# A two-layer hybrid step on Trainium2: the second unit's first experts found in two halves of eight, the samples' gate moved between the halves of the first unit, and query products cut in two

## The chip, the cores and the metric

One core of a Trainium2 chip runs the whole program. The metric is the device time of one execution in microseconds (us); lower is better.

## The reference

Two layers run over 256 prompt tokens and 8 sample tokens, 1024 features each. A layer is a state-space branch and an attention branch mixed by two gates, and then a retrieval of single experts ("PEER"). Cut to what matters here:

```python
x = x + (ga * ya + gb * yb) @ w_out
h = rmsnorm(x, norm_ffn)
for head in range(8):
    q = h @ wq[head]                       # 256 columns, two halves of 128
    s1, s2 = q[:, :128] @ keys[head, 0].T, q[:, 128:] @ keys[head, 1].T
    sc1, i1 = top_k(s1, 16); sc2, i2 = top_k(s2, 16)
    cand = sc1[:, None] + sc2[None, :]      # 16 x 16 sums
    sc, sel = top_k(cand, 16)
    idx = i1[sel // 16] * 128 + i2[sel % 16]
    act = gelu(sum(u[idx] * h)) * softmax(sc)
    out += act @ v[idx]
x = x + out
```

The rows u[idx] and v[idx] stand side by side in one table, 2048 float32 numbers (8 KB) for one expert.

## The kernel before

All five engines run straight programs written out by hand, one layer after the other; semaphores are the only order between them. No planner is at work. In a layer come first the projections, the state-space scan and the attention. Then comes the expert stage, which this change is about.

**Slots.** The expert stage is cut into units: one (token tile, head) pair of 128 tokens each, eight heads for tile 0, eight for tile 1, and one short unit for the samples. A unit has 16 slots, the last one 8, so that a layer has 264 slots. For slot n, POOL issues one gather (line 2506) that brings one expert row for each of 128 tokens, 1 MB in all, into place n % 8 of a ring of 8 (`ring`). DVE multiplies the u half with the tokens and sums (`inputs`, line 1843), ACT takes the gelu of the 128 sums (line 2228), DVE builds a small diagonal matrix from it (`diagonal`, line 1852), and PE adds diagonal times v half to sums that stay in PSUM banks for a whole tile (`outputs`, line 1195). The gather of slot n waits until `outputs(n - 8)` has run. DVE's loop takes the work of slot n in this order: `inputs(n)`, `diagonal(n - 1)`, at a unit's start `weights(u)`, then some steps of the generator `best_experts(u + 1)`, which finds the 16 experts of the next unit, then what `late_tiles(n)` holds.

**What else runs beside the slots.** The query products of the heads and their scores against the keys stand in a table of steps, `projection_steps` (line 77). Behind `outputs(n)` PE runs `STEPS[n]`: `queries` (8 matmuls with 264 columns, line 530), `scores` (line 1082) or `rows` (transposes of the normed rows of tile 1 and of the samples, line 539). ACT copies their result from PSUM in its own slot loop, behind `gelu(n)`, from `STEPS[n - 2]`, or `STEPS[n - 4]` for n under 8. So ACT, and with it gelu(n + 1) and `diagonal(n + 1)`, waits where PE is not through with the product. Where both have 4 PSUM banks each, `wide` are those that ACT empties and `aux` those that DVE empties.

**The start of the stage.** The first unit cannot be prepared beside slots. DVE finds its experts alone in `first_experts` (lines 1731 to 1759): eight from the best 8 x 8 candidates, whose number lets slot 0 start, then eight more from 16 x 16. Then it adds `out(0, 1)` to tile 1, forms the samples' gate (`sample_gated`, lines 1585 and 1587), adds `out(1, 1)` and copies the samples' partial sums (line 1242). PE needs the gate for `out_samples` (line 1042), behind which come `out(2, 1)`, the two sums over the samples' parts (line 1141) and `out(3, 1)`. POOL's gathers of slots 4 and 5 wait for `out_samples(0)`, those of slots 6 and 7 for `out(2, 1)` and `out(3, 1)`, whose weights lie where these slots' rows go. `outputs(0)` waits until DVE has read all of these banks, in its slot 4. In slots 6 and 7 DVE forms the norm of tile 1 and of the samples (`px_mean`, and `px_rows`, line 1672); the steps `rows` on PE wait for it. The second unit's experts come from the general `best_experts(1)`, whose 16 numbers appear together, in slot 11.

## Time and profile before

| what | value |
|---|---|
| median of 3 runs | 2105.01 us (2101.08 to 2106.8) |
| the profiled execution | 2099.31 us |
| its span, first to last instruction | 2097.5 us |
| PE, DVE, ACT, POOL busy | 79%, 69%, 23%, 32% |
| gathers (line 2506) | 528 of 1 MB |
| mean DMA rate over the span | 356 GB/s |
| mean granted TensorE clock | 0.823 |

The span is cut into stages by what DMA carries. A layer's expert stage starts with its first gather, at 361.2 us in layer 0 and at 1402.7 us in layer 1, and ends some 14 us behind its last gather, issued at 1031.3 us and at 2072.7 us. Busy shares over the whole span mix these stages with the others, so the stage has to be looked at by itself, window by window.

### The profile page before, as it was taken

What the parts mean: (1) busy time and instruction counts of PE and PEld (TensorE: products, weight loads), DVE (VectorE), ACT (ScalarE), POOL (GpSimd) and SP (SyncE); (2) the same over time, 40 slices, a digit from 0 to 9 for tenths busy, and PEclk for the clock granted to TensorE, in tenths of its full rate; (3) what the DMA queues carried; (4) which work ended last, traced back from release to release, by engine and by line L of the source; (5) the groups of instructions that cost most, each with busy time, mean ns of one, the idle gap of its engine ahead of it and who ended that gap; (6) DMA issues with size and microseconds to landing.
All of it is one profiled execution on the core that took longest, in us unless ns stands there. A gap on an engine that the chain in (4) does not pass through costs nothing. (4 is left out here: it accounts for less than half of the span.)

```text
span 2097.5 us, 29681 instructions
## 1 busy us (share of the span) xinstructions
PE 1662.4 (79%) x10874; PEld 839.5 (40%) x10874; DVE 1446.4 (69%) x3630; ACT 489.6 (23%) x1422; POOL 676.2 (32%) x614
## 2 busy tenths in 40 slices
PE   7999999878787666666699999998787776666665
PEld 6888677433333111111178876764332321111110
DVE  3557544778778878778736565347887888787787
ACT  2346211211211221111222543112112112111112
POOL 0011000354544454444300110014444454444442
PEclk9999999887887676666799999998887876666667
DMA  5568897999999999999954688978999999999997
GB/s 181 189 205 302 302 393 279 351 397 421 415 421 421 405 421 421 420 417 412 383 175 155 215 323 293 389 288 351 405 417 416 417 420 409 421 421 418 417 415 319
DMA packets 136004, 746.76 MB, mean 356 GB/s; under 512 B 16692, under 2 KB 17309, under 8 KB 57763
## 3 DMA queue, kind: packets, MB, share of 16 engines
q0 software_dynamic: 84416, 587.50, 68.8%
q1 hardware_dynamic: 51442, 157.37, 20.9%
q8 instruction: 86, 1.41, 0.3%
q14 instruction: 60, 0.48, 0.1%
HBM read 733.48 MB, written 11.52 MB: 355 GB/s over the span
## 5 line engine op out<-in xcount | busy, mean ns | idle before, releaser
L1195 PE MATMUL ps<-arena 64*64 64x512 f32 x4096 | 750.6, 832 | 371.0 <-DVE arena L1852 369.4
L2506 POOL DMA_INDIRECT arena<-in_peer_uv,arena x528 | 628.3, 1190 | 777.4 <-PE ps L1195 619.5
L1843 DVE CUSTOM_DVE_ANT_0 arena<-arena,h 128x1024 f32<-128x1024 f32 x512 | 627.1, 1225 | 216.0 <-DMA arena<-in_peer_uv,arena 208.9
L1195 PEld LDWEIGHTS ps<-arena 64*64 64x64 f32 x4096 | 140.8, 166 | 919.0 <-DVE arena L1852 864.8
L530 PE MATMUL ps<-ht_tok,wring 128*128 128x264 f32 (+1 forms) x1472 | 346.8, 395 | 4.2 <-DMA wring<-in_w_in 2.8
L2228 ACT ACTIVATE arena<-arena 128x1 f32<-128x1 f32 x528 | 105.2, 203 | 969.9 <-DVE arena L1843 968.3
L530 PEld LDWEIGHTS ps<-ht_tok,wring 128*128 128x128 f32 x1472 | 281.2, 194 | 68.8 <-issue 15.8
L1852 DVE TENSOR_SCALAR arena<-consts,arena 128x64 f32<-128x64 f32 (+1 forms) x528 | 164.6, 312 | 38.8 <-ACT arena L2228 35.3
L530 PE MATMUL ps<-arena,wring 128*128 128x264 f32 x256 | 63.9, 393 | 3.2 <-DVE arena L1522 3.2
L530 PE MATMUL ps<-ht_tok,arena 128*128 128x264 f32 (+2 forms) x280 | 60.4, 373 | 1.4 <-DVE ht_tok L1715 1.4
L530 PE MATMUL ps<-arena,gate 128*128 128x256 f32 x256 | 59.1, 383 | 0.0
L530 PEld LDWEIGHTS ps<-ht_tok,arena 128*128 128x128 f32 x280 | 47.6, 208 | 25.5 <-issue 17.8
L2483 POOL DMA_DIRECT2D nrow<-in_norm_ffn x2 | 1.1, 534 | 175.2 <-PE ps L897 175.2
L2228 ACT ACT_TABLE_LOAD x40 | 51.3, 1283 | 0.9
L530 PEld LDWEIGHTS ps<-arena,gate 128*128 128x128 f32 x256 | 47.2, 189 | 9.8 <-issue 3.4
L530 PEld LDWEIGHTS ps<-arena,wring 128*128 128x128 f32 x256 | 46.2, 190 | 11.1 <-DVE arena L1522 3.5
L2469 POOL DMA_DIRECT2D out<-h x16 | 8.5, 534 | 119.9 <-DVE h L1435 119.9
L530 PE MATMUL ps<-wring,ht_tok 128*128 128x272 f32 (+2 forms) x192 | 42.8, 379 | 1.7 <-DVE ht_tok L2553 1.7
L2221 ACT ACT_TABLE_LOAD x34 | 43.6, 1283 | 0.8
L1843 DVE DVE_READ_ACCUMULATOR2_ANT arena<- 128x1 f32 x528 | 43.4, 82 | 0.0
L2192 ACT COPY gate<-ps 128x264 f32<-128x264 f32 (+2 forms) x40 | 13.4, 335 | 126.1 <-PE ps L530 126.1
L530 PEld LDWEIGHTS ps<-wring,ht_tok 128*128 128x128 f32 x192 | 34.7, 201 | 10.9 <-issue 3.4
(388 smaller groups left out, 1738.2 us busy)
## 6 DMA issues: line engine op xcount, KB each, us to landing
arena<-in_pages SPq DMA_DIRECT2D x256, 272.0 KB, 6.2
wring<-in_w_in SPq DMA_DIRECT2D x36, 1024.0 KB, 5.1
arena<-in_peer_uv,arena POOLq DMA_INDIRECT x528, 12.5
h<-in_state_ssm POOLq DMA_DIRECT2D x16, 512.0 KB, 6.4
out<-h POOLq DMA_DIRECT2D x16, 512.0 KB, 6.1
wring<-in_w_ssm_proj SPq DMA_DIRECT2D x8, 1024.0 KB, 11.4
arena<-in_w_out SPq DMA_DIRECT2D x8, 1024.0 KB, 8.7
arena<-in_peer_wq SPq DMA_DIRECT2D x6, 1024.0 KB, 10.6
```

The source lines that it names most:

```text
L530: last = pe.matmul(dst, w(c), rhs(c), start=start and c == 0, stop=stop and c == chunks - 1)
L1195: last = pe.matmul(ps[to:to + 64, SUM_BANK[t] + i, :], diag[rows, n % DIAGS, 0:64], ring[rows, HOME[n % RING], cols], start=n in TILE_FIRS ...
L1843: dve.tensor_tensor_reduce(ring[:, HOME[k], 0:D_MODEL], ring[:, HOME[k], 0:D_MODEL], tokens, 1.0, 0.0, ALU.mult, ALU.add, dots[:, column(n ...
L1852: dve.tensor_scalar(diag[:, n % DIAGS, 0:outs], table[:, 0:outs], gel[:, column(n)], wexp[:, column(n)], ALU.mult, ALU.mult).then_inc(sem( ...
L2192: wide.emptied(act.copy(gate[:, 2 * hh + m, lo:hi], ps[:, b, 0:hi - lo]))
L2221: act.activation(w, w, ACT.Exp, accum_out=wsum[:, u % 2:u % 2 + 1]).then_inc(sem("experts_exp"), 1)
L2228: act.activation(gel[:, at:at + 1], dots[:, at:at + 1], ACT.Gelu).then_inc(sem("gelu_ready"), 1)
L2469: pool.dma_start(h1[b], places[b % PLACES]).then_inc(sem(f"state_store{b % PLACES}"), 16)
L2483: pool.dma_start(nrow[:, :], of_layer("norm_ffn", layer).partition_broadcast(P)).then_inc(sem("ffn_row_load"), 16)
L2506: pool.indirect_dma_start(ring[:, HOME[k], :], None, table, bass.IndirectOffsetOnAxis(ap=idx[:, TOPK * u + j:TOPK * u + j + 1], axis=0)).t ...
```

## The change

It does five things.

1. `first_experts` becomes a generator, `early_experts(u)`, used for units 0 and 1. For unit 0, `out(0, 1)` and `sample_gated` run between its two halves. The copies of line 1242 move into DVE's slots 0 and 1.
2. On PE the two sums over the samples' parts (`samples_summed`) run behind `outputs(0)`, so that `out(3, 1)` follows `out(2, 1)` directly, and `outputs(0)` waits for `out(3, 1)` alone. DVE adds `out(2, 1)` and `out(3, 1)` in its slots 2 and 3, the samples' sums in slot 4. The banks of the tiles' sums change to fit.
3. Unit 1's experts are found as unit 0's: eight, whose numbers release slots 16 to 23, then eight more for slots 24 to 31. DVE takes 6 steps in slots 8 and 9 and 4 in each slot from 10 to 31, except none in 16 to 18; it was 4 in slots 7 to 11, then 3.
4. The first steps on PE stand later: head 1's queries behind slots 2 and 3 (were 0 and 1), its scores behind 4 (2), `rows` behind 11 to 13 (8 to 10), head 2's queries behind 14 and 15 (12 and 13) and its scores behind 17 (15). `px_mean` moves from DVE's slot 6 to 7, `px_rows` from 7 to 10. ACT reads `STEPS[n - 3]` for n under 8.
5. Each query product of heads 3 to 7 is cut in two: four of its eight matmuls behind the slot where the product stood, the other four behind the next. ACT copies the result one slot later. The scores stay behind the slot they had.

The core of the diff:

```diff
-SUM_BANK = (4, 6, 4)
+SUM_BANK = ((5, 6), (7, 4), (5, 6))
...
-    steps = {0: [("queries", 1, 0, 0, P)], 1: [("queries", 1, 1, 0, P)], 2: [("scores", 1, (0,))]}
+    steps = {2: [("queries", 1, 0, 0, P)], 3: [("queries", 1, 1, 0, P)], 4: [("scores", 1, (0,))]}
     for first in range(3):
-        steps[8 + first] = [("rows", first)]
+        steps[11 + first] = [("rows", first)]
...
-        at = (2, 6, 10) if hh > 2 else (12, 13, 15)
+        at = (2, 6, 10) if hh > 2 else (14, 15, 17)
+        for m in range(2):
+            if hh > 2:
+                steps[begun + at[m]] = [("queries_begun", hh, m)]
+            steps[begun + at[m] + (hh > 2)] = [("queries", hh, m, 0, TOKENS)]
...
+            def queries_begun(hh, m):
+
+                w = query_weights(hh, m)
+                b = wide.fill()
+                product(ps[:, b, 0:TOKENS], w, lambda c: ht[:, c, :], DC // 2, stop=False)
...
+                if n == 0:
+                    samples_summed()
...
-            first_experts()
-            out(0, 1)
-            sample_gated()
+            for said in early_experts(0):
+                if said == "first found":
+                    out(0, 1)
+                    sample_gated()
             out(1, 1)
-            ahead = best_experts(1)
-            for half in range(2):
-                copy4(hp[2][:, half * 512:(half + 1) * 512])
+            ahead = early_experts(1)
...
-                elif n == 6:
+                elif n == 7:
                     px_mean(1, slice(46, 48))
-                elif n == 7:
+                elif n == 10:
                     px_rows((1, 2))
...
-                for _ in range(0 if n < 7 or n in (TOPK, TOPK + 1) else 4 if n < 12 else 3):
+                for _ in range(0 if n < 8 or TOPK <= n < TOPK + 3 else 6 if n < 10 else 4 if n < 2 * TOPK else 3):
                     next(ahead, None)
...
-                for step in STEPS.get(n - 2 if n >= 8 else n - 4, ()):
+                for step in STEPS.get(n - 2 if n >= 8 else n - 3, ()):
...
-                if n in (0, TOPK // 2):
+                if u < 2 and n % (TOPK // 2) == 0:
                     pool.wait_ge(sem("idx_ready"), since("idx_ready") + 1 + n // (TOPK // 2))
                 elif j == 0:
-                    pool.wait_ge(sem("idx_ready"), since("idx_ready") + u + 2)
+                    pool.wait_ge(sem("idx_ready"), since("idx_ready") + u + 3)
```

The first place is on PE in layer 0, from the samples' parts to the first transposes of later rows. Four matmuls of line 1195 (1221 in the changed file) are one slot; 128x128 with one line of their own are the transposes, 8 or 2 in a row are queries and scores. Before:

```order
L1042 MATMUL ps<-arena,gate 32x256 x32
L530 MATMUL ps<-arena,gate 128x256 x8
L1141 MATMUL ps<-h,consts 8x512 x2
L530 MATMUL ps<-arena,gate 128x256 x8
L1195 MATMUL ps<-arena 64x512 x4
L530 MATMUL ps<-ht_tok 128x128 x8
L1195 MATMUL ps<-arena 64x512 x4
L530 MATMUL ps<-ht_tok 128x128 x8
L1195 MATMUL ps<-arena 64x512 x4
L1082 MATMUL ps<-arena,gate 128x128 x2
L1195 MATMUL ps<-arena 64x512 x24
L539 MATMUL ps<-consts,h 128x128
```

After the change:

```order
L1044 MATMUL ps<-arena,gate 32x256 x32
L532 MATMUL ps<-arena,gate 128x256 x16
L1221 MATMUL ps<-arena 64x512 x4
L1168 MATMUL ps<-h,consts 8x512 x2
L1221 MATMUL ps<-arena 64x512 x8
L532 MATMUL ps<-ht_tok 128x128 x8
L1221 MATMUL ps<-arena 64x512 x4
L532 MATMUL ps<-ht_tok 128x128 x8
L1221 MATMUL ps<-arena 64x512 x4
L1103 MATMUL ps<-arena,gate 128x128 x2
L1221 MATMUL ps<-arena 64x512 x28
L541 MATMUL ps<-consts,h 128x128
```

The second `out` product joins the first, the two 8x512 sums stand behind slot 0, head 1's products move by two slots, and seven slots instead of six stand between head 1's scores and the first transposes, which are then behind slot 11.

The second place is on DVE, around the norm of tile 1 and of the samples (line 1672, 1702 in the changed file), which the transposes need; line 1843 (1886) is a slot's input product and line 1852 (1895) its diagonal. Before:

```order
L1843 ISA arena<-arena,h 128x1024
L1843 ISA arena 128x1
L1852 TENSOR_SCALAR arena<-consts,arena 128x64
L1774 MAX arena<-arena 128x8 x2
L1778 MAX_INDEX arena<-arena 128x8 x2
L1783 MATCH_REPLACE arena<-arena 128x128 x2
L1774 MAX arena<-arena 128x8 x2
L1670 RECIPROCAL st<-st 128x2
L1672 SCALAR_TENSOR_TENSOR h<-x,st,nrow 128x1024 x2
L1843 ISA arena<-arena,h 128x1024
L1843 ISA arena 128x1
L1852 TENSOR_SCALAR arena<-consts,arena 128x64
```

After the change:

```order
L1776 MAX arena<-arena 128x8 x2
L1780 MAX_INDEX arena<-arena 128x8 x2
L1783 TENSOR_SCALAR arena<-arena,layer_off 128x8
L1784 CAST arena<-arena 128x8
L1786 TENSOR_TENSOR arena<-arena 128x256
L1788 MATCH_REPLACE arena<-arena 128x256
L1791 MAX arena<-arena 128x8
L1700 RECIPROCAL st<-st 128x2
L1702 SCALAR_TENSOR_TENSOR h<-x,st,nrow 128x1024 x2
L1886 ISA arena<-arena,h 128x1024
L1886 ISA arena 128x1
L1895 TENSOR_SCALAR arena<-consts,arena 128x64
```

Before, the norm stands behind four steps of the second unit's search, in slot 7; now it stands in slot 10, behind the whole first half of that search (slots 8 and 9) and four steps of its second half.

The third place is on PE, from head 2's scores (128x128 x4) to head 3's scores. Before:

```order
L1082 MATMUL ps<-arena,gate 128x128 x4
L1195 MATMUL ps<-arena 64x512 x12
L530 MATMUL ps<-ht_tok,arena 128x264 x8
L1195 MATMUL ps<-arena 64x512 x16
L530 MATMUL ps<-ht_tok,arena 128x264 x8
L1195 MATMUL ps<-arena 64x512 x16
L1082 MATMUL ps<-arena,gate 128x128 x4
```

After the change:

```order
L1103 MATMUL ps<-arena,gate 128x128 x4
L1221 MATMUL ps<-arena 64x512 x4
L532 MATMUL ps<-ht_tok,arena 128x264 x4
L1221 MATMUL ps<-arena 64x512 x4
L532 MATMUL ps<-ht_tok,arena 128x264 x4
L1221 MATMUL ps<-arena 64x512 x12
L532 MATMUL ps<-ht_tok,arena 128x264 x4
L1221 MATMUL ps<-arena 64x512 x4
L532 MATMUL ps<-ht_tok,arena 128x264 x4
L1221 MATMUL ps<-arena 64x512 x12
L1103 MATMUL ps<-arena,gate 128x128 x4
```

The number of matmuls is the same; a slot's four stand between the two halves of each product.

## Rows read from the trace of the kernel before

**Rows 1.** The page, part 2: mean busy share of the DMA engines in 40 slices, in tenths

```profile
DMA  5568897999999999999954688978999999999997
```

**Rows 2.** Windows: start:end, length, busy us (count) of PE, PEld, DVE, ACT, POOL, clock, DMA, GB/s

```profile
368.00:372.00 4.00, 4.00 (x48) 2.12 (x44) 0.76 (x2) 0.67 (x1) 0.82 (x1) 0.57 1.00 397
378.00:386.00 8.00, 7.40 (x46) 5.13 (x48) 7.01 (x17) 0.61 (x4) 2.70 (x3) 1.00 0.78 272
408.00:418.00 10.00, 10.00 (x41) 4.36 (x41) 7.18 (x18) 4.36 (x10) 6.71 (x5) 0.59 0.71 252
430.00:452.00 22.00, 16.64 (x92) 8.42 (x96) 19.14 (x52) 2.24 (x11) 9.40 (x7) 0.92 1.01 422
452.00:464.00 12.00, 7.95 (x64) 2.31 (x56) 9.50 (x28) 4.50 (x11) 9.87 (x9) 1.00 0.91 331
1449.00:1457.00 8.00, 8.00 (x33) 2.60 (x33) 6.32 (x16) 4.36 (x10) 4.91 (x4) 0.50 0.67 242
```

**Rows 3.** Timeline of POOL: gathers of slots 8, 16, 32, 34 [idle <-releaser]

```profile
384.79 0.94 POOL L2506 DMA_INDIRECT arena<-in_peer_uv,arena  x1 [1.29 <-PE ps L1195]
...
408.74 1.68 POOL L2506 DMA_INDIRECT arena<-in_peer_uv,arena  x1 [8.73 <-DVE arena L1816]
...
453.58 1.90 POOL L2506 DMA_INDIRECT arena<-in_peer_uv,arena  x1 [0.30 <-issue]
...
457.87 1.67 POOL L2506 DMA_INDIRECT arena<-in_peer_uv,arena  x1 [0.30 <-issue]
```

**Rows 4.** Line 2506, windows 453:454 and 457:458: issue to landing of slots 32 and 34

```profile
DMA to landing us min/median/max: 6.5/6.5/6.5
...
DMA to landing us min/median/max: 8.6/8.6/8.6
```

**Rows 5.** Timeline of PE, same columns, layer 0

```profile
367.79 5.35 PE L1042 MATMUL ps<-arena,gate 128*32 128x256 f32 x64 [2.45 <-DVE gate L1587]
...
401.38 1.99 PE L1195 MATMUL ps<-arena 64*64 64x512 f32 x8 [2.61 <-DVE arena L1852]
403.30 1.91 PE L539 MATMUL ps<-consts,h 128*128 128x128 f32 x6
...
415.65 4.08 PE L530 MATMUL ps<-ht_tok,wring 128*128 128x264 f32 x16
...
445.26 4.63 PE L530 MATMUL ps<-ht_tok,arena 128*128 128x264 f32 x16
...
473.56 5.83 PE L530 MATMUL ps<-ht_tok,arena 128*128 128x264 f32 x16
```

**Rows 6.** Timeline of DVE, same columns, layer 0

```profile
357.07 0.49 DVE L1740 MAX8 arena<-arena 128x8 f32<-128x128 f32 x2 [5.75 <-ACT arena L2205]
...
366.80 0.23 DVE L1759 TENSOR_SCALAR arena<-arena 128x16 f32<-128x16 f32 x1
...
391.18 0.49 DVE L1774 MAX8 arena<-arena 128x8 f32<-128x128 f32 x2 [0.74 <-ACT arena L2205]
...
393.73 2.48 DVE L1672 SCALAR_TENSOR_TENSOR h<-x,st,nrow 128x1024 f32<-128x1024 f32 x2
...
408.39 1.22 DVE L1843 CUSTOM_DVE_ANT_0 arena<-arena,h 128x1024 f32<-128x1024 f32 x1
...
409.76 1.22 DVE L1843 CUSTOM_DVE_ANT_0 arena<-arena,h 128x1024 f32<-128x1024 f32 x1
...
428.13 0.49 DVE L1774 MAX8 arena<-arena 128x8 f32<-128x128 f32 x2 [1.39 <-ACT arena L2205]
...
444.06 1.22 DVE L1843 CUSTOM_DVE_ANT_0 arena<-arena,h 128x1024 f32<-128x1024 f32 x1
...
450.44 0.32 DVE L1852 TENSOR_SCALAR arena<-consts,arena 128x64 f32<-128x64 f32 x1 [2.41 <-ACT arena L2228]
```

**Rows 7.** Timeline of ACT around the exponents of the second unit

```profile
409.51 1.28 ACT L2221 ACT_TABLE_LOAD   x1
410.81 0.22 ACT L2221 ACTIVATE arena<-arena 128x16 f32<-128x16 f32 x1
```

More of the change, by code:

```diff
@@ L1045, in out_samples, with query_part, query_weights @@
                 marks["sums", pair] = marks["sums"] = aux.n
-            def queries(hh, m, lo, hi):
+            def query_part(hh, m, c):
+                w = state["wq", hh]
+                rows = w[:, c] if hh != 6 else wq_high[:, c] if c < 3 else wq_late[:, c - 3]
+                return rows[:, m * P:(m + 1) * P]
+            def query_weights(hh, m):
                 if m == 0:
@@ L1137, in tensor_layer, with samples_summed @@
             out(2, 1)
-            pe.wait_ge(sem("aux_free"), since("aux_free") + 4 + marks["sums"])
-            for half in range(2):
-                b = aux.fill()
-                aux.filled(pe.matmul(ps[0:SAMPLES, b, :], cst("sel8"), hp[2][:, half * 512:(half + 1) * 512], start=True, stop=True))
             out(3, 1)
             marks["x", 1] = aux.n
+            def samples_summed():
+                pe.wait_ge(sem("aux_free"), since("aux_free") + 4 + marks["sums"])
+                for half in range(2):
+                    b = aux.fill()
+                    assert b not in SUM_BANK[0]
+                    aux.filled(pe.matmul(ps[0:SAMPLES, b, :], cst("sel8"), hp[2][:, half * 512:(half + 1) * 512], start=True, stop=True))
+                marks["x", 2] = aux.n
             def next_rows(t):
@@ L1750, in first_experts @@
                         then(dve.match_replace(sums, ctop[:, 0:8], sums, -3e38))
+                    yield
                     eight = slice(8 * k, 8 * k + 8)
                     then(dve.max(ctop[:, eight], sums))
+                    yield
                     then(dve.max_index(ctopi[:, eight], ctop[:, eight], sums))
-                    first_rows(k, n)
+                    yield
+                    yield from eight_rows(u, k, n)
+                    yield
                     if k == 0:
@@ L2237, in late_tiles @@
                 if n == 5:
-                    act.wait_ge(sem("aux_free"), since("aux_free") + 4 + marks["x", 1])
+                    act.wait_ge(sem("aux_free"), since("aux_free") + 4 + marks["x", 2])
                     squares(hp[1], x[:, 1, :], st[:, 46:47])
```

65 lines of the change are left out of this document (40 added, 25 removed).

## The prediction

> **What bounds the kernel now.** I read the page's slices first. Where the expert stage runs, the DMA engines are busy for nine tenths or more of nearly every slice, and the slices at the stage's start are lower [rows 1]. So the time of this stage is the bytes that its gathers bring, at the rate that DMA reaches, plus the holes in which DMA has too little queued. The windows size both. In an undisturbed stretch DMA moves 422 GB/s at a share of 1.01 (window 430:452) [rows 2], so a gather of 1 MB takes 2.48 us. Against that rate three stretches of layer 0 lack transfer: 378 to 386 moves 272 GB/s, a loss of 8 x (1 - 272/422) = 2.8 us; 408 to 418 moves 252, a loss of 4.0; 452 to 464 moves 331, a loss of 2.6 [rows 2]. That is 9.4 us in a layer. Layer 1 shows the same holes, such as 3.4 us in 1449 to 1457 [rows 2]. Everything that the change touches lies in this start of the stage. Past slot 34 nothing is to be had, and what the change can bring at most is 2 x 9.4 = 19 us.
>
> Then I read who makes each hole. For the first it is PE: slot 4's gather waits for the first of the samples' parts, which PE began at 367.79 after 2.45 us of waiting for the gate, and slot 8's leaves only at 384.79 [rows 3, 5]. For the second it is DVE: slot 16's gather waits 8.73 us for the index list [rows 3]. For the third it is PE, with a query product of 4.63 us in front of slot 23's output (445.26); ACT waits for it and DVE for ACT, 2.41 us at 450.44 [rows 5, 6]. The question is whether a hole closes or moves, so I follow each chain up to slot 34, which lands at 457.87 + 8.6 = 466.5 today [rows 3, 4].
>
> **Gate and first experts.** The gate no longer waits for the second half of the first unit's search. It is ready at some 362.3, and PE goes from `out(1, 1)` straight on at 365.4, 2.4 sooner. The samples' parts took 5.35 us in a stretch with a granted clock of 0.57 [rows 2, 5], that is partly at 1.2 GHz, after the wait that now goes. Their cost lies between 5.35 and, at 2.4 GHz throughout, 5.35 x 0.57 = 3.1. I take 3.7, since PE comes out of continuous work. The two sums behind slot 0 take 1.9 us more off the way. `outputs(0)` can then start at about 377, and gather 8 leaves near 378.5, 6 us sooner. The first hole closes, since DMA then always has a gather to work on, and at 2.48 us each slots 6, 7 and 8 land near 383, 385.5 and 388. At this point the change is 2.8 us ahead. `out(0, 1)` and the gate delay the second eight experts by 0.9 us. Their gathers leave 20 us later, so that costs nothing.
>
> **Slots 5 to 8.** Head 1's products are two slots later, so the earlier slots bring little here. The mean of tile 1's squares follows slot 7's input, which waits for its landing, and ACT then goes through two table loads of 1.28 us [rows 7] before it copies head 1's scores. I get 391.0 for DVE's first search step, against 391.18 [rows 6]. What could be gained by being sooner is spent here. The rows show no pause behind a table load: the load at 409.51 ends at 410.79 and the exponential starts at 410.81 [rows 7]. The Trainium skill (ScalarE: Activation LUTs, "What ACT_TABLE_LOAD costs") has some 1.38 us of drain on top of 1.28 us for each switch. By that, four switches in this stretch and at the second unit's exponentials would put 5.5 us more on each layer, about 2119 in all; this trace shows none of it, and I go by the rows.
>
> **The second unit's search.** Today DVE works without a pause from 391.18 to 409.76: five slots of 1.37 us (the distance of 408.39 and 409.76), the norm with its reciprocal, 2.65, the rest, 9.1, for the search [rows 6]. Searched in two halves as unit 0 (357.07 to 366.80) it costs 9.8 [rows 6], 0.7 more. With slot 8's input done while DVE waits, the new stretch is 391.0 + 4 x 1.37 + 2.65 + 9.8 = 408.9 up to slot 13, where today it is at 409.76. The first eight numbers come in slot 9, near 396.5, so gather 16 leaves when slot 8's output is through, about 397 in place of 408.74 [rows 3]. The second hole is gone, and DMA is nearly 7 us ahead.
>
> **What is late next.** The norm now comes in slot 10. Behind it stand two slots (2.7) and seven of the 24 steps (2.9) before 408.9, so it ends near 403.4. Today it ends at 396.2 [rows 6]. PE has almost nothing to do between. The transposes wait for slot 11's diagonal (about 408) and its output, and begin at some 410.0, against 403.30 [rows 5]. From there to the second unit's scores in DVE's hands it is 428.13 - 403.30 = 24.8 us today, with seven outputs in it [rows 5, 6]. Now there are six. I take off 1.5 (an output is 1.99 for two records at the low clock, 1.1 at the high one) and add 0.8, since gelu(12) waits for the second unit's exponentials, which come a slot later. That gives 434.1 for the third unit's search, 6.0 later than 428.13. DVE has then one slot more behind it: 15.9 us from there to slot 24's input today, 14.5 now. Slot 24's input starts at 448.6 against 444.06 [rows 6]. DVE, not DMA, sets slots 18 to 24, and the lead of 7 us is gone.
>
> **The cut products.** No matmul is added, and ACT waits less, as the result is read a slot later. In front of slot 23's output stand now some 2 us of product instead of 4.63. Slot 22's output ends near 449.6, half a product at 451.7, slot 23's output at 452.8, the other half at 454.7, slot 24's output at 455.8. Gather 32 leaves at 456.0, 2.4 later than 453.58 [rows 3], and lands 6.5 later [rows 4] at 462.5, against 460.1. Its followers are ready at once. If they follow without the hole of today, slot 34 lands at 467.5, 1.0 late; if the hole stays, 2.4 late. I take 1.5. The later cut products (slots 34 to 86) run while DMA has gathers queued at its full rate, and cost and bring nothing. If that queue were short, each would be worth up to the 2.41 of row 450.44. The moved banks, the one more wait of POOL and the later read of head 2's weights (head 7's load follows it by 50 slots) are hidden by the same queue.
>
> **Sum.** +1.5 us in each layer, +3 in all: 2099.3 + 3 = 2102.3 for an execution like the profiled one. That one is 5.7 under the median of 2105.0. On the median's scale I predict **2108**. A measurement of this kernel can tell about 0.3%, 6.3 us, from no change.
>
> **Rival 1: no measurable change (likeliest).** The chain above, with errors of 3 us a layer: 2102 to 2114. For it speaks that PE and DVE carry nearly the same work between slots 8 and 24 as before, and that DMA is starved whatever they finish late.
>
> **Rival 2: faster, 2093.** PE does its outputs and transposes between 405 and 421 at the high clock. Five outputs at 1.1 in place of 1.99 give 4.4 us, and 5.1 us of transposes at half the time 2.5, so the third unit's search starts near 427, ahead of today's. Gather 32 then leaves near 449 and lands near 455.5, and slot 34 near 460.5 instead of 466.5: -6 a layer, -12 in all, 2105 - 12 = 2093. Against it: the stretch has a clock of 0.59 today [rows 2] although PE is busy throughout.
>
> **Rival 3: slower, 2115.** PE rests longer ahead of the transposes than today (from 396 to 408 three outputs), so the low clock lasts into head 2's products. At the low clock a pair of those products costs 5.83 instead of 4.08 (the pairs at 473.56 and 415.65) [rows 5]. Two of them add 3.5 us to the search's start, every one of which reaches gather 32, as the queue is empty by then. 1.5 + 3.5 = 5 a layer, +10 in all: 2115. It decides from the point at which the third unit's search starts after 436. The Trainium skill (TensorE: Matmul & The Clock Gate, "Part 1: The HAM clock gate") says that the default state is throttled and that activity releases it; this rule speaks against making PE wait, and the windows agree, with 1.00 in 378:386 and 0.50 to 0.59 behind PE's rests.
>
> **How the numbers follow.** No change 0.44, faster 0.28, slower 0.28. Beyond the three mechanisms there are the bounds: the samples' parts at 5.35 cost 1.7 us that the wait for slot 7 hides; closing all holes would give 2086, which needs DVE and PE to gain 5 us that I don't find. The range for eight in ten is 2092 to 2119; the likeliest case alone has 2102 to 2114.
>
> **What would show it.** Right: slot 8's gather near 378.5 and no hole at 378 to 386; gather 16 near 397; the norm of line 1672 (now 1702) ending near 403.5; the first transposes near 410; the third unit's search near 434; gather 32 near 456; DMA shares under 0.95 spread between 413 and 460. Wrong: a third search that starts before 430, a clock near 1 from 408 on, or DMA at 420 GB/s from 386 to 470.

## The result and the profile after

| | before | changed |
|---|---|---|
| median of 15 runs each | 2103.06 us (2098.87 to 2107.66) | 2110.66 us (2105.24 to 2115.44) |
| ratio to before | | 1.0035, 95% interval 1.0025 to 1.0044 |
| the profiled execution | 2099.31 us | 2111.16 us |
| its span | 2097.5 us | 2109.1 us |

The changed kernel is slower by 7.6 us. This is just outside the 0.3% that I called no change, and the interval lies on both sides of that bound. The two profiled executions differ by 11.9 us, which is more than the medians do, since the one of before was a short one.

The slices of the changed kernel look as before at the start of the stage in layer 0, where one slice is lower [rows 1]:

```profile
DMA  5468897989999999999954689979999999999997
```

The windows tell more. The columns are those of [rows 2]:

```profile
378.00:386.00 8.00, 6.57 (x44) 2.86 (x44) 6.50 (x13) 2.18 (x6) 4.60 (x4) 1.00 1.01 425
396.00:408.00 12.00, 4.46 (x24) 0.61 (x16) 11.55 (x37) 1.69 (x3) 3.08 (x3) 0.59 1.02 421
408.00:418.00 10.00, 9.69 (x37) 3.29 (x37) 8.01 (x22) 3.19 (x9) 3.69 (x3) 0.50 0.88 344
418.00:430.00 12.00, 12.00 (x56) 7.42 (x56) 3.40 (x8) 0.97 (x4) 3.61 (x3) 0.83 0.77 268
430.00:445.00 15.00, 10.63 (x72) 5.13 (x72) 11.23 (x42) 2.04 (x8) 4.68 (x5) 1.00 1.00 402
445.00:452.00 7.00, 4.33 (x20) 1.81 (x13) 6.90 (x14) 0.61 (x3) 1.98 (x2) 0.56 0.80 294
452.00:464.00 12.00, 11.72 (x85) 5.17 (x83) 7.40 (x18) 4.84 (x12) 5.80 (x5) 0.97 0.74 253
```

The first hole is closed: 425 GB/s in place of 272. The second hole has moved rather than gone. DMA is at full rate to 408 and then lacks, against 422 GB/s, 10 x (1 - 344/422) = 1.8 us, 12 x (1 - 268/422) = 4.4 us, and later 0.7, 2.1 and 4.8 us. That is 13.8 us, against the 9.4 of the three holes before. So some 4 us of transfer time more are lost in this layer than before, and they are lost after slot 16.

Who makes these holes stands in the timelines, with columns as in [rows 3]. On POOL, the gathers of slots 0, 8, 16, 18 and 32 and the small load ahead of the last:

```profile
362.74 1.00 POOL L2550 DMA_INDIRECT arena<-in_peer_uv,arena  x1 [32.03 <-DVE arena L1764]
...
381.32 0.94 POOL L2550 DMA_INDIRECT arena<-in_peer_uv,arena  x1 [1.70 <-PE ps L1221]
...
397.30 1.89 POOL L2550 DMA_INDIRECT arena<-in_peer_uv,arena  x1 [1.38 <-DVE arena L1764]
...
407.75 1.08 POOL L2550 DMA_INDIRECT arena<-in_peer_uv,arena  x1 [5.85 <-PE ps L1221]
...
458.08 0.55 POOL L2549 DMA_DIRECT2D nrow<-in_norms  x1 [2.36 <-issue]
458.93 1.74 POOL L2550 DMA_INDIRECT arena<-in_peer_uv,arena  x1 [0.30 <-issue]
```

On DVE, the start of the second unit's search, the norm, the start of the third unit's search, slot 24's input and the diagonal that waits longest behind it:

```profile
391.37 0.48 DVE L1776 MAX8 arena<-arena 128x8 f32<-128x128 f32 x2
...
401.56 2.48 DVE L1702 SCALAR_TENSOR_TENSOR h<-x,st,nrow 128x1024 f32<-128x1024 f32 x2
...
433.64 0.49 DVE L1817 MAX8 arena<-arena 128x8 f32<-128x128 f32 x2 [2.75 <-ACT arena L2247]
...
448.21 1.22 DVE L1886 CUSTOM_DVE_ANT_0 arena<-arena,h 128x1024 f32<-128x1024 f32 x1
...
457.01 0.31 DVE L1895 TENSOR_SCALAR arena<-consts,arena 128x64 f32<-128x64 f32 x1 [3.48 <-ACT arena L2270]
```

On PE, the samples' parts, slot 10's output, the first transposes, head 2's first product, and head 3's second product in its two halves with the outputs around them:

```profile
366.81 3.67 PE L1044 MATMUL ps<-arena,gate 128*32 128x256 f32 x64
...
405.46 1.98 PE L1221 MATMUL ps<-arena 64*64 64x512 f32 x8 [4.80 <-DVE arena L1895]
...
410.23 1.91 PE L541 MATMUL ps<-consts,h 128*128 128x128 f32 x6
...
420.87 4.37 PE L532 MATMUL ps<-ht_tok,wring 128*128 128x264 f32 x16
...
448.26 1.98 PE L1221 MATMUL ps<-arena 64*64 64x512 f32 x8 [2.67 <-DVE arena L1895]
450.17 3.29 PE L532 MATMUL ps<-ht_tok,arena 128*128 128x264 f32 x8
453.39 1.09 PE L1221 MATMUL ps<-arena 64*64 64x512 f32 x8
454.41 2.05 PE L532 MATMUL ps<-ht_tok,arena 128*128 128x264 f32 x8
```

Gather 16 is out at 397.30, but the gathers behind it need slot 10's output, which waits 4.80 us for a DVE that is in the norm. So the released list of slots 16 to 23 is of no use from slot 18 on.

A layer's first gather is issued some us sooner or later from one profiled execution to the next (361.21 to 368.00 in layer 0 of before and the thirteen others), in a stage that no edit touches. So I compare kernels by times **after the layer's first gather**. Each number below is one row's start less that of the first gather; "length" is from the first to the last gather of the stage. Layer 0 / layer 1:

| kernel | gather 8 | 2nd search | norm ends | gather 16 | transposes | 3rd search | gather 32 | length |
|---|---|---|---|---|---|---|---|---|
| before | 23.6 / 23.6 | 30.0 / 30.0 | 35.0 / 35.0 | 47.5 / 47.5 | 42.1 / 42.1 | 66.9 / 66.7 | 92.4 / 92.1 | 670.0 / 670.0 |
| changed | 18.6 / 18.8 | 28.6 / 30.3 | 41.3 / 43.0 | 34.6 / 36.2 | 47.5 / 49.2 | 70.9 / 73.1 | 96.2 / 98.7 | 674.4 / 676.9 |
| late_alone | 23.6 / 23.6 | 30.0 / 30.0 | 45.8 / 45.8 | 47.5 / 47.5 | 50.8 / 50.8 | 70.3 / 70.3 | 95.4 / 95.6 | 673.1 / 674.9 |
| cut_alone | 21.9 / 23.6 | 28.3 / 30.0 | 33.3 / 35.0 | 45.8 / 47.5 | 40.4 / 42.1 | 64.8 / 66.8 | 88.6 / 92.2 | 667.6 / 670.9 |
| norm_early | 18.4 / 17.9 | 28.8 / 28.2 | 34.0 / 33.4 | 38.2 / 37.6 | 40.6 / 40.0 | 65.3 / 64.5 | 91.6 / 90.7 | 669.4 / 668.4 |
| uncut | 18.9 / 18.0 | 30.5 / 28.5 | 43.2 / 41.2 | 36.5 / 34.4 | 49.4 / 47.4 | 73.6 / 72.2 | 99.2 / 98.3 | 677.6 / 677.2 |
| gate_alone | 18.2 / 19.7 | 26.4 / 28.8 | 31.4 / 33.8 | 44.0 / 46.3 | 38.5 / 40.9 | 63.2 / 66.2 | 88.6 / 91.8 | 666.5 / 670.2 |
| gate_halves_cut | 18.9 / 18.0 | 31.1 / 28.6 | 31.2 / 28.7 | 41.2 / 38.7 | 40.3 / 37.9 | 65.1 / 63.3 | 88.9 / 88.8 | 666.8 / 666.8 |

From gather 32 to the last gather all of them take 577.6 to 579.3 us. So the queue is full from there on, and every us at gather 32 reaches the end. The change is late there by 3.8 and 6.6 us, and long by 4.4 and 6.9. The sum, 11.3, is nearly the 11.6 by which the two spans differ; outside the two stages the executions differ by +1.5, -0.7 and -0.5 us, which nearly cancel. So within the stage the time is lost between gathers 16 and 32, in both layers.

### The profile page after: what moved, and what is told of

Read it like the earlier page. It is cut to its first block, busy times and chain, and to the rows that moved or that the text cites. A ratio compares the mean times of both kernels' runs of the same rounds, so it can differ in the third digit from the quotient of the medians.

```text
span 2109.1 us, 29703 instructions
## 1 busy us (share of the span) xinstructions
PE 1669.4 (79%) x10874; PEld 836.1 (40%) x10874; DVE 1448.0 (69%) x3650; ACT 490.1 (23%) x1422; POOL 672.0 (32%) x614
## 4 chain that ended last, share of the span: by engine, by line
PE 39%; DMA 29%; DVE 15%; issue 13%; ACT 2%; POOL 1%; SPq 1%; DVEq 0%; POOLq 0%; ACTq 0%
DMA arena<-in_peer_uv,arena 25%; PE ps L532 23%; PE ps L1221 7%; PE ps L541 2%; DVE arena L1895 2%; DVE arena L1821 2%; DVE arena L1886 2%; DMA arena<-in_pages 1%; DMA wring<-in_w_in 1%; POOL arena L2550 1%; DVE arena L1817 1%; PE ps L984 1%; PE ps L959 1%; DVE arena L1838 1%; DVE arena L1826 1%
## 5 line engine op out<-in xcount | busy, mean ns | idle before, releaser
L532 PE MATMUL ps<-ht_tok,wring 128*128 128x264 f32 (+1 forms) x1472 | 351.1, 396 | 4.5 <-DMA wring<-in_w_in 3.5
L2095 ACT ACTIVATE arena<-nrow,late 128x128 f32<-128x128 f32 x128 | 39.0, 390 | 0.0
L532 PEld LDWEIGHTS ps<-wring,ht_tok 128*128 128x128 f32 x192 | 33.8, 196 | 9.7 <-issue 2.5
## 6 DMA issues: line engine op xcount, KB each, us to landing
wring<-in_w_ssm_proj SPq DMA_DIRECT2D x8, 1024.0 KB, 11.6
arena<-in_peer_wq SPq DMA_DIRECT2D x6, 1024.0 KB, 10.7
```

The source lines that it names most:

```text
L532: last = pe.matmul(dst, w(c), rhs(c), start=start and c == 0, stop=stop and c == chunks - 1)
L2095: last = act.activation(stx[:, s % 2, c, :], brow[:, s, :], ACT.Copy, scale=dtx3[:, c, s:s + 1])
```

## The experiments

The rival explanations were these. The late norm (A): the norm in slot 10 holds up transposes, head 2's products and the third unit's search. The cut products (B): they cost more than they save. The work before slot 8 costs (C). The clock of PE behind its rests (F). And for the gate (G): whether the closed first hole is kept to the end. The expectations name further letters where they need them. Every kernel is a variant of one of the two, timed against before on its own chip; ratios are to before.

**late_alone**: before, with the late norm and what follows from it, and nothing else of the change. What follows from it is a group: the later places of the transposes and of head 2's products and scores, one slot more without search steps, and 4 steps in a slot up to 31 instead of 3.

```diff
-        steps[8 + first] = [("rows", first)]
+        steps[11 + first] = [("rows", first)]
-        at = (2, 6, 10) if hh > 2 else (12, 13, 15)
+        at = (2, 6, 10) if hh > 2 else (14, 15, 17)
-                elif n == 7:
+                elif n == 10:
-                for _ in range(0 if n < 7 or n in (TOPK, TOPK + 1) else 4 if n < 12 else 3):
+                for _ in range(0 if n < 7 or TOPK <= n < TOPK + 3 else 4 if n < 2 * TOPK else 3):
```

> The kernel before, with only the later norm and its followers taken from the change: px_rows in slot 10, transposes behind slots 11 to 13, head 2's products behind 14 and 15, its scores behind 17, no search steps in slots 16 to 18 and 4 in each slot from 19 to 31. Theory A (the late norm starves PE, then DVE works the third unit's search late): slower by 6 to 16 us than before, the third unit's search starting 4 to 8 us later, gather 32 later by 3 to 8 us in each layer, with the second hole (408 to 418) as before or wider. Theory B (the cut products are what costs): within 4 us of before. Theory C (the work before slot 8 costs): within 4 us of before.

Measured: 2110.78 us, ratio 1.0030 (1.0016 to 1.0043). Its norm and its third unit's search, on DVE:

```profile
409.38 2.48 DVE L1672 SCALAR_TENSOR_TENSOR h<-x,st,nrow 128x1024 f32<-128x1024 f32 x2
...
436.37 0.49 DVE L1774 MAX8 arena<-arena 128x8 f32<-128x128 f32 x2 [2.76 <-ACT arena L2205]
```

With the first gather at 366.10, the third search starts at 70.3 in both layers, 3.4 and 3.6 later than before, and gather 32 leaves 3.0 and 3.5 later. I had expected 4 to 8 us at the search; the ratio, 6.3 us, is at the low end of the 6 to 16 that I expected. The late norm with its group costs 0.30% by itself, which is almost the size of the change's 0.35%. But the change also holds the gate, which alone gains 0.42% (gate_alone below), so the single parts don't add up to it: about 0.47% comes only with the parts together.

A part of that shows on PE. The first transposes and head 2's first product here, and a window:

```profile
416.91 1.70 PE L539 MATMUL ps<-consts,h 128*128 128x128 f32 x6
...
424.14 3.83 PE L530 MATMUL ps<-ht_tok,wring 128*128 128x264 f32 x16
```

```profile
418.00:430.00 12.00, 12.00 (x66) 6.96 (x67) 7.16 (x16) 2.18 (x8) 6.40 (x6) 1.00 0.99 395
```

The transposes begin 3.3 and 1.6 us later than the change's, but PE has a granted clock of 0.96 from 416 to 436, and from the first transposes to the third search it is 19.5 us in both layers. In the change, with the same work on PE in the same order, it is 23.4 and 23.9 at a clock of 0.74 (410 to 433). So late_alone is spared some 4 us a layer that the change pays, and its search starts as early from later transposes. Before pays them too (0.74 from 403 to 428), so against before this is no loss of the change's; rather late_alone's 0.30% is less than a late norm costs where the clock stays as in before. No run shows how much of the 4 us would reach the end.

**cut_alone**: before, with the products of heads 3 to 7 in two halves (part 5 of the change, as in its diff) and nothing else.

> The kernel before, with only the query products of heads 3 to 7 cut in two. Theory A: within 4 us of before, or faster by up to 5 us, since the wait of 2.4 us in front of slot 23's output becomes shorter. Theory B: slower by 5 to 10 us, with the wait at head 3's second product moved or longer. Theory C: within 4 us of before.

Measured: 2102.11 us, ratio 1.000 (0.9987 to 1.0014). Its samples' parts and the second half of head 3's second product on PE:

```profile
369.40 3.67 PE L1044 MATMUL ps<-arena,gate 128*32 128x256 f32 x64 [2.45 <-DVE gate L1610]
...
446.94 2.05 PE L532 MATMUL ps<-ht_tok,arena 128*128 128x264 f32 x8
```

The cut costs nothing, and B falls. Nor does it bring anything that the time shows. Layer 0 looks 2.4 us shorter than before, but 1.7 of them are there at gather 8, ahead of any cut product: the samples' parts took 3.67 us instead of 5.35 in this execution. Between gathers 8 and 32 another 2.0 us are gained in layer 0, where the diagonal that waits 2.41 us in before waits 0.62. In layer 1, where it waits 2.19 and the first half of the product runs 2.73 us instead of 2.05, gather 8 leaves at 23.6 as before, and gather 32 too leaves as before (92.2 against 92.1).

**norm_early**: the change, with the norm in slot 8 behind the search's first six steps.

```diff
-        steps[11 + first] = [("rows", first)]
+        steps[9 + first] = [("rows", first)]
-        at = (2, 6, 10) if hh > 2 else (14, 15, 17)
+        at = (2, 6, 10) if hh > 2 else (12, 13, 15)
-                elif n == 10:
+                elif n == 8:
-                for _ in range(0 if n < 8 or TOPK <= n < TOPK + 3 else 6 if n < 10 else 4 if n < 2 * TOPK else 3):
+                for _ in range(0 if n < 8 or TOPK <= n < TOPK + 2 else 6 if n < 10 else 4 if n < 2 * TOPK else 3):
```

> The changed kernel, with the norm back in slot 8, the transposes behind slots 9 to 11, head 2's products behind 12 and 13, its scores behind 15, search steps excluded in slots 16 and 17 only. Theory A: the lead of the sooner gate and of the first eight experts is kept, gather 32 leaves 6 to 10 us sooner than in the changed kernel, and the time falls 12 to 20 us under the changed kernel's, 4 to 12 us under the kernel before. Theory B: within 4 us of the changed kernel. Theory C: within 4 us of the changed kernel.

Measured: 2101.54 us, ratio 0.9992 (0.9980 to 1.0004), 0.43% under the change. Its first transposes on PE, and its gather 32 on POOL:

```profile
405.52 1.91 PE L541 MATMUL ps<-consts,h 128*128 128x128 f32 x6
```

```profile
456.44 1.74 POOL L2550 DMA_INDIRECT arena<-in_peer_uv,arena  x1 [0.30 <-issue]
```

The sooner norm, with the steps behind it, gives back the whole loss, as A says. The gain over before that I had expected (4 to 12 us) is missing: the third search starts 1.6 us sooner than before in layer 0, and gather 32 only 0.8 sooner. Against the change gather 32 leaves 4.6 and 8.0 us sooner, where I had expected 6 to 10.

**uncut**: the change, with whole products again.

```diff
-            if hh > 2:
-                steps[begun + at[m]] = [("queries_begun", hh, m)]
-            steps[begun + at[m] + (hh > 2)] = [("queries", hh, m, 0, TOKENS)]
+            steps[begun + at[m]] = [("queries", hh, m, 0, TOKENS)]
```

> The changed kernel with whole query products again in heads 3 to 7, all else kept. Theory A: within 4 us of the changed kernel, or up to 6 us slower. Theory B: 5 to 10 us faster than the changed kernel, back at the time of before. Theory C: within 4 us of the changed kernel.

Measured: 2114.32 us, ratio 1.0050 (1.0033 to 1.0066), beside 1.0035 of the change. The longest wait of its diagonals in this stretch is 4.01 us, where the change has 3.48:

```profile
460.24 0.31 DVE L1889 TENSOR_SCALAR arena<-consts,arena 128x64 f32<-128x64 f32 x1 [4.01 <-ACT arena L2264]
```

Inside the change the cut helps a little, if anything (the intervals overlap). Its own cost is not the cause of the loss.

**early_three**: norm_early, with 3 steps of the search in a slot from 16 on, as before, instead of 4.

```diff
-                for _ in range(0 if n < 8 or TOPK <= n < TOPK + 2 else 6 if n < 10 else 4 if n < 2 * TOPK else 3):
+                for _ in range(0 if n < 8 or TOPK <= n < TOPK + 2 else 6 if n < 10 else 4 if n < TOPK else 3):
```

> The kernel of the run norm_early, with three search steps in each slot from 18 on in place of four. Theory A1 (with four steps the search ends sooner, DVE runs slots 24 to 28 at 1.4 us each, and PE and ACT cannot follow at head 3's second product): the wait of 3.1 us there becomes under 1, gather 32 leaves 2 to 4 us sooner after the first gather (91.6 us in norm_early), and the time falls 2 to 6 us under norm_early's. Theory D (the remaining loss comes from PE's low clock between slots 8 and 14 alone): within 2 us of norm_early.

Measured: 2098.13 us, ratio 0.9971 (0.9958 to 0.9985). With 4 steps a slot is longer, the third search is over sooner, and the slots from 24 on, at 1.37 us each, run into head 3's second product. The longest wait there is 2.27 us, after 3.07 in norm_early:

```profile
454.15 0.32 DVE L1895 TENSOR_SCALAR arena<-consts,arena 128x64 f32<-128x64 f32 x1 [2.27 <-ACT arena L2270]
```

The wait is shorter, but not under 1 us as expected, and gather 32 leaves at 91.7 in both layers, not sooner than norm_early's. So the time is 0.2% better with intervals that only just overlap, and where it comes from stays open.

**norm_first**: early_three, with the norm ahead of the search's steps in slot 8, and the transposes behind slots 8 to 10.

```diff
-        steps[9 + first] = [("rows", first)]
+        steps[8 + first] = [("rows", first)]
...
-                elif n == 8:
-                    px_rows((1, 2))
...
+                if n == 8:
+                    px_rows((1, 2))
```

> The kernel of the run early_three, with the norm ahead of slot 8's search steps and the transposes behind slots 8 to 10. Theory A (what counts is when PE can begin the transposes and head 2's products): the third unit's search starts 2 to 4 us sooner after the first gather than in norm_early (65.3 us there), the first eight experts come 2.6 us later and cost nothing, and the time is 2 to 5 us under early_three's. If the eight experts count instead (theory E), the hole before slot 16 opens again and the time is the same or 2 to 5 us longer than early_three's.

Measured: 2095.95 us, ratio 0.9972 (0.9954 to 0.9989). The transposes begin at 37.2 in both layers and gather 32 leaves at 89.8 and 88.9, 2 to 3 us sooner than before's. The third search starts at 64.3 and 65.1, where I had expected 2 to 4 us less than norm_early's 65.3, and by the time it is level with early_three, not 2 to 5 us better. With the norm ahead, the halves are no loss.

**gate_alone**: parts 1 and 2 of the change alone, that is the gate between the halves of the first unit's search and the sums behind slot 0. The places of the steps, `best_experts(1)` and the whole products are those of before.

```diff
-            first_experts()
-            out(0, 1)
-            sample_gated()
+            for said in early_experts(0):
+                if said == "first found":
+                    out(0, 1)
+                    sample_gated()
             out(1, 1)
             ahead = best_experts(1)
...
+                if n == 0:
+                    samples_summed()
```

> The kernel before, with the change's first two parts alone: the gate between the two halves of the first unit's search, the copies in DVE's slots 0 and 1, out(3, 1) right behind out(2, 1), the sums behind slot 0. Theory A: the first hole (378 to 386) closes and gather 8 leaves some 5 us sooner after the first gather, but DVE's stretch up to slot 13 stays, so that gather 32 leaves 0 to 3 us sooner than before (92.4) and the time is within 5 us of before, at most 5 us faster. Theory G (the closed hole is kept to the end): 5 to 6 us faster than before.

Measured: 2096.02 us, ratio 0.9958 (0.9944 to 0.9971). Three windows of it, at the places of the three holes:

```profile
379.00:387.00 8.00, 6.55 (x41) 2.84 (x39) 6.24 (x13) 1.36 (x5) 2.31 (x2) 1.00 1.01 427
```

```profile
408.00:418.00 10.00, 10.00 (x42) 4.36 (x42) 7.21 (x18) 4.36 (x10) 6.72 (x5) 0.60 0.72 252
452.00:464.00 12.00, 7.77 (x64) 2.31 (x56) 9.41 (x28) 4.34 (x10) 9.87 (x9) 0.99 0.93 329
```

This is the lowest ratio of all, though its interval overlaps with those of early_three, norm_first and the two kernels that follow: 0.42% under before and 1.0035 / 0.9958 = 0.8% under the change. The first hole is closed, the second and third stand as they were (252 and 329 GB/s, against 252 and 331 in [rows 2]), and the lead is kept: everything from the second search to the last gather is 3.5 to 3.8 us sooner in layer 0. So the closed first hole does reach the end, if the search starts sooner with it. In layer 1 the lead at gather 8 is 3.8, but shrinks to 1.2 at the second search and to nothing at the end of the stage. 0.42% are 8.8 us, more than either theory said and more than the two layers of this one execution show, which was the slowest of its five; where the rest comes from is left open.

**gate_cut**: gate_alone with the cut products, whose edit is that of cut_alone.

> The kernel of gate_alone with the cut products added. If the two gains add up (the lead of 3.6 us a layer from the closed first hole, and up to 2.4 us a layer that the profile of cut_alone showed and its median did not): 9 to 14 us under before. If the cut brings nothing (cut_alone's median): within 2 us of gate_alone, which was 8.8 us under before by its ratio.

Measured: 2096.66 us, ratio 0.9978 (0.9958 to 0.9997). Gather 32 leaves at 89.2 and 89.0 and the stage is 667.0 and 667.6 long. No gain over gate_alone shows (the intervals overlap): the cut brings nothing here either.

**gate_halves_cut**: gate_cut with the second unit searched in halves, the norm in slot 7 ahead of the search, 6 steps in slots 7 and 8, 4 up to 15, none in 16 and 17, then 3.

```diff
-            ahead = best_experts(1)
+            ahead = early_experts(1)
...
-                elif n == 7:
-                    px_rows((1, 2))
...
+                if n == 7:
+                    px_rows((1, 2))
-                for _ in range(0 if n < 7 or n in (TOPK, TOPK + 1) else 4 if n < 12 else 3):
+                for _ in range(0 if n < 7 or n in (TOPK, TOPK + 1) else 6 if n < 9 else 4 if n < TOPK else 3):
```

> The kernel of gate_cut with the second unit's experts found in two halves as the change does, but with head 1's products left behind slots 0 to 2, and the norm in slot 7 ahead of the search (6 steps in slots 7 and 8, then 4, from 18 on 3). Theory A (the late norm was the fault of the change, not the halves): the hole at 408 to 418 closes, the third unit's search starts no later after the first gather than in gate_cut, and the time is 2 to 8 us under gate_cut's. If the halves themselves cost (0.7 us of DVE and the order of its work): the same as gate_cut or up to 4 us slower.

Measured: 2096.37 us, ratio 0.9968 (0.9956 to 0.9981). Gathers 16 and 32 on POOL (the first gather is at 365.04), and two windows:

```profile
406.26 1.93 POOL L2550 DMA_INDIRECT arena<-in_peer_uv,arena  x1 [2.27 <-PE ps L1221]
...
453.96 0.98 POOL L2550 DMA_INDIRECT arena<-in_peer_uv,arena  x1 [0.30 <-issue]
```

```profile
410.00:420.00 10.00, 10.00 (x43) 4.51 (x43) 8.23 (x21) 4.36 (x10) 5.07 (x4) 0.62 0.95 351
454.00:466.00 12.00, 6.45 (x52) 2.10 (x48) 8.47 (x25) 2.61 (x7) 8.32 (x8) 0.97 1.01 420
```

Gather 16 is no longer held by the list, and leaves 2.9 and 5.1 us sooner than in gate_cut, the kernel that it starts from. But gather 32 leaves where gate_cut's does (88.9 and 88.8 against 89.2 and 89.0), and the third search starts at 65.1 and 63.3 against 63.7 and 63.5, later in layer 0, where I had expected it no later. The expected 2 to 8 us don't show either. Transfer is lost elsewhere instead: 387 to 400 moves 340 GB/s, where gate_cut has 391, and 420 to 432 moves 350. So what gather 16 gains is spent again by gather 32, as if the hole before slot 16 were not on the path but PE's and DVE's chain up to slot 32. The norm stands ahead of the search here too, so this run doesn't test the halves alone. Its interval overlaps with those of gate_alone and gate_cut, so no order among the three is shown.

**warm**: the change, with extra products of 264 columns on PE behind the outputs of slots 7 to 10, whose results nobody reads.

```diff
+WARM = {7: 3, 8: 8, 9: 22, 10: 7}
...
+                elif n in WARM:
+                    b = wide.fill()
+                    for _ in range(WARM[n]):
+                        pe.matmul(ps[:, b, 0:TOKENS], ident, ht[:, 0, :], start=True, stop=True)
```

> The changed kernel, with 3, 8, 22 and 7 extra products of 264 columns behind the outputs of slots 7 to 10, whose results nobody reads, so that PE has work between 396 and 408. Theory F (the low clock behind PE's rest is a large part of the loss): the granted clock stays at 2.4 GHz through the transposes and head 2's products, the third unit's search starts 4 to 7 us sooner after the first gather than in the changed kernel (70.9 us), gather 32 leaves 3 to 6 us sooner (96.2), and the time falls 6 to 12 us. If the clock matters little (theory A without it): within 3 us of the changed kernel, or slower by what the extra products add.

Measured: 2116.24 us, ratio 1.0058 (1.0044 to 1.0072). The last 17 extra products behind slot 9 and the first transposes on PE, and a window ahead of them:

```profile
409.81 7.73 PE L1248 MATMUL ps<-ht_tok,consts 128*128 128x264 f32 x34
...
422.82 1.59 PE L542 MATMUL ps<-consts,h 128*128 128x128 f32 x6
```

```profile
401.00:413.00 12.00, 11.32 (x57) 8.12 (x58) 11.52 (x39) 1.89 (x4) 2.84 (x2) 1.00 1.02 421
```

The clock does stay at its higher level, 1.00 where the change has 0.59, and the transposes take 1.59 us instead of 1.91 and the outputs 1.09 instead of 1.98. From the first transposes to the third search it is 19.3 us instead of 23.4, close to late_alone's 19.5. But an extra product takes 7.73 / 17 = 0.45 us (two records each), twice what I had sized, so that the transposes begin 7.3 us later, and the search 3.3 us later where I had expected 4 to 7 sooner. The trade brings no gain; the ratio is above the change's, with intervals that touch.

**warm_half**: the same with about half as many extra products.

```diff
-WARM = {7: 3, 8: 8, 9: 22, 10: 7}
+WARM = {7: 1, 8: 4, 9: 11, 10: 3}
```

> The changed kernel with half the extra products of the run warm: 1, 4, 11 and 3 behind the outputs of slots 7 to 10. In warm they took twice the time I had sized them at, and held slot 10's output back by 7 us; yet the clock stayed at 2.4 GHz, and from the first transposes to the third unit's search it was 19.3 us against 23.4 in the changed kernel. Theory F: the transposes begin as in the changed kernel (47.5 us after the first gather, at most 1 us later), the search starts 3 to 5 us sooner than 70.9, and the time falls 3 to 8 us under the changed kernel's. Without F: within 3 us of it.

Measured: 2107.55 us, ratio 1.0023 (1.0009 to 1.0036). Three windows:

```profile
396.00:408.00 12.00, 10.17 (x55) 6.23 (x48) 11.45 (x40) 0.41 (x2) 5.88 (x5) 1.00 1.01 422
411.00:421.00 10.00, 9.04 (x43) 3.77 (x42) 9.00 (x23) 3.08 (x9) 5.63 (x4) 0.79 0.97 371
418.00:430.00 12.00, 12.00 (x46) 6.11 (x46) 4.93 (x12) 1.57 (x6) 2.86 (x3) 0.63 0.84 312
```

The first gather is 3.05 us later here than in the change, so 411 to 421 answers to the change's 408 to 418, and it moves 371 GB/s instead of 344. But the clock does not stay: from 418 to 430 it is 0.63, head 2's first product takes 5.76 us where the change has 4.37, and the third search starts at 71.4, no sooner than the change's 70.9, where I had expected 3 to 5 us. In layer 1 it starts at 70.7 (the change: 73.1). The ratio is lower than the change's, with intervals that overlap. So these two kernels don't give the clock's time back. At the third search it is some 4 us a layer by the rows of late_alone and warm; what it is worth in the time stays open.

**head1_early**: the change, with head 1's products, scores and the mean of the squares where before has them.

```diff
-    steps = {2: [("queries", 1, 0, 0, P)], 3: [("queries", 1, 1, 0, P)], 4: [("scores", 1, (0,))]}
+    steps = {0: [("queries", 1, 0, 0, P)], 1: [("queries", 1, 1, 0, P)], 2: [("scores", 1, (0,))]}
...
-                elif n == 7:
+                elif n == 6:
```

> The changed kernel with head 1's products back behind slots 0 and 1 and its scores behind slot 2, px_mean in slot 6. If head 1's later place is what spends the lead of the first hole (theory H): the second unit's search starts 1.5 us or more sooner after the first gather than in the changed kernel (28.6 us), and the time falls 3 to 7 us. If the search waits for slot 7's gelu and its table load anyway: within 2 us of the changed kernel.

Measured: 2114.71 us, ratio 1.0053 (1.0038 to 1.0068). The expectation was missed, and on ACT one sees why:

```profile
386.56 0.27 ACT L2234 COPY gate<-ps 128x128 f32<-128x128 f32 x1 [5.30 <-PE ps L532]
...
389.56 0.27 ACT L2234 COPY gate<-ps 128x128 f32<-128x128 f32 x1 [2.63 <-PE ps L532]
```

ACT still reads `STEPS[n - 3]`, so it asks for each product one slot sooner than in gate_alone, which reads `n - 4`, and stands still for it. The squares of tile 1 come behind it, 25.2 us after the first gather instead of 21.6, and the second search starts at 31.3 and 32.8 instead of 28.6 and 30.3. So head 1's places and ACT's reading distance belong together. This kernel doesn't test the first without the second.

## Why the prediction was right, and where it was not

The time was 2110.66 us, for 2108 predicted and a range of 2092 to 2119. The likeliest case was no measurable change, by a bound of 0.3%, in 2102 to 2114; the change is slower by 0.35%, just beyond that bound. The sum had a loss of 3 us and the measured one is 7.6. The predicted time is closer than that by luck: I added to 2105.0, the median of three runs, and the median of fifteen is 2103.06, so 1.9 us of the missing loss were in the base. The chain up to slot 24 is that of the case; behind it a term failed.

**Gate and first experts: right.** The samples' parts take 3.67 us (taken: 3.7). Gather 8 leaves 18.6 us behind the first gather (from my numbers 378.5 - 361.2 = 17.3), 5.0 sooner than before, and the first hole is gone.

**Slots 5 to 8: right for the change, but not the last word.** The search starts at 391.37, forecast 391.0. The stage's first gather is 1.5 us later in this execution, so that it is 1.3 sooner after it than before; in layer 1 it is 0.3 later. "What could be gained by being sooner is spent here" holds for this change, which moves head 1's products by two slots and the search to slot 8; gate_alone moves neither and has 3.6 us of lead in layer 0 and 1.2 in layer 1. Which of the two spends it, no run separates. I had not asked what the first part would give by itself. The table loads cost no more than the rows said:

```profile
409.75 1.28 ACT L2270 ACT_TABLE_LOAD   x1
411.04 0.29 ACT L2270 ACTIVATE arena<-arena 128x1 f32<-128x1 f32 x2
```

The function behind the load starts 0.01 us after its end. The drain of 1.38 us that the Trainium skill has (ScalarE: Activation LUTs, "What ACT_TABLE_LOAD costs") is not seen here either.

**The second unit's search and what is late next: right.** Gather 16 at 397.3 (397), the norm's end at 404.0 (403.4), the first transposes at 410.2 (410.0), the third search at 433.6 (434.1), slot 24's input at 448.2 (448.6). DVE and PE set slots 18 to 24, as said, and the lead at slot 16 is spent on them. That all these times fit within 0.6 us is in part luck, since this execution's stage began 1.5 us later than the one that I counted from. After the first gather I had the transposes at 48.8 and the third search at 72.9; layer 0 has 47.5 and 70.9, layer 1 has 49.2 and 73.1. late_alone and norm_early show from both sides that the late norm with its group costs; the search's 4 steps in a slot belong to that group.

**The cut products: this term of the sum failed.** I gave slot 24's input to gather 32 7.4 us; it took 458.93 - 448.21 = 10.7, where before takes 9.5. Of the 3.3 us missed, 1.0 are slot 22's output, which waited 2.67 us for DVE, then ran at 1.98 instead of 1.09, and ended 2.0 us behind slot 24's input where I had 1.0. Another 1.1 are the first half product, 3.29 us instead of 2.05, in a window with a clock of 0.56. And 1.4 lie on POOL, between slot 24's output (456.39 + 0.94) and the gather, where the small load `nrow<-in_norms` stands; I had let the gather follow in 0.2. The other steps took 0.2 less than I gave them. So a good part of the miss is the lower clock behind a rest of PE, which I had left out of this term. "ACT waits less" was wrong as well, against before: slots 24 and on take 1.37 us each, reach the product sooner than it is done, and a diagonal waits 3.48 us, after 2.41 before [rows 6]. With whole products it waits 4.01 (uncut).

The next line of that step failed too: of 2.4 us at gather 32 I let 0.9 be won back by slot 34. Nothing is. The windows have 4.8 us of hole in 452 to 464, where there were 2.6 [rows 2], and what is late at gather 32 is late at the end. Forecast was +1.5 us in each layer. The medians have 7.6 / 2 = 3.8, and the two profiles 4.4 and 6.9.

**Rival 3** put the loss into head 2's products at the low clock, from a third search after 436. In layer 0 it started at 433.6, and head 2's first product took 4.37 us, near the 4.08 of before [rows 5]; in layer 1 it took 4.89. So against before the mechanism added little there and bit elsewhere: at head 3's half product, behind a rest of 2.67 us. Its rule, that activity gives the clock (the Trainium skill, TensorE: Matmul & The Clock Gate, "Part 1: The HAM clock gate"), is borne out by warm, with 1.00 where the change has 0.59. **Rival 2** did not come: 408 to 418 has a clock of 0.50. Its size was wrong too. It took 4.4 us off the outputs and halved the transposes' 5.1; at the higher clock, in warm, these take 1.59 + 1.59 + 1.09 = 4.3, and the whole stretch to the third search is some 4 us shorter in late_alone and warm, not 6.9.

## What to carry to other kernels

A hole in DMA is worth closing only if the chain that refills the ring behind it comes sooner too: closing the first hole was worth 0.42% by itself, while narrowing the second showed no gain, since PE and DVE set the next sixteen slots. Parts that were measured one by one need not add up: the late norm's +0.30% and the gate's -0.42% stand in a change of +0.35%. When work is moved to release something early, look at the work that is pushed behind it (here one norm of 2.65 us, three slots later), and price it at the first place where the queue is full for good. Predict each part of a bundle by itself, and compare profiles from the start of the stage that is touched, not from the start of the program.

## What the runs showed of the hardware that I had not expected

- The samples' parts on PE, behind a wait of 2.45 us, took 5.35 us in both layers of before and of late_alone and in layer 1 of cut_alone, and 3.67 us in layer 0 of cut_alone. Where the gate is early and PE doesn't wait, they took 3.67 us in both layers of all eleven profiles. So the wait was followed by the slower run in five of six stretches, and the gain of 1.7 us comes with the wait's end.
- A rest of 2.67 us on PE was followed by one output of 1.98 us and a half product of 3.29 us; the next half product took 2.05 again.
- 264 columns of float32 cost 0.45 us on PE at a granted clock of 1.00, and the 16 records of a product 3.83 us, so that keeping PE awake with them is dear.
- The first stage's start differs by up to 7 us between profiled executions, through stages that no edit touches.
- The stretch from the first transposes to the third search took 19.5 and 19.3 us at a granted clock of 0.96 and 1.00 (late_alone, warm) and 23.4 us at 0.74 (the change), for the same work on PE.
